# Odd attention: the query norm as scale and bias of the exponential, per partition, instead of spread over the heads' dimensions

## What is computed

```python
def rms_norm(x, g):
    return x * rsqrt(mean(x * x, -1) + EPS) * g

q, k = rms_norm(q, g_q), rms_norm(k, g_k)          # over the 64 dimensions of a head
score = einsum(relu(qi . ki), wi)                  # a small indexer
idx = top_k(score, 256)                            # the keys that a query may see
logits = einsum(q, k[idx]) * 64 ** -0.5            # 8 query heads, 2 key heads
p = softmax(where(sel_ok, logits, NEG))
out = einsum(p, v[idx])
```

## Time and profile before

| | us |
|---|---|
| median of 3 runs | 2625.73 (2623.49 to 2625.83) |
| profiled execution, its own time | 2626.03 |
| its span | 2624.2 |
| PE busy | 2550.2 (97%) |
| DVE busy | 1195.1 (46%) |
| POOL busy | 1087.1 (41%) |
| ACT busy | 598.9 (23%) |

### The profile page before, as it was taken

The page is one execution under the profiler, slowest core; times in us unless marked ns, Lnnn a source line. Parts: engine busy times, 40 slices in busy tenths (PEclk is TensorE's granted clock), DMA queues, the critical chain, the costliest instruction groups (busy, mean ns, idle before and its releaser), DMA issues.

```text
span 2624.2 us, 38744 instructions
## 1 busy us (share of the span) xinstructions
PE 2550.2 (97%) x16483; PEld 2413.7 (92%) x16483; DVE 1195.1 (46%) x1582; ACT 598.9 (23%) x889; POOL 1087.1 (41%) x899
## 2 busy tenths in 40 slices
PE   7999999999999999999989999989999999999998
PEld 7998866999999999999969987669999999999998
DVE  4224389443333323333568876663433343333324
ACT  3200178211001000010248801651200100001000
POOL 5242256344443344443342333953544334443331
PEclk8999999999999999999999998999999999999999
DMA  5111120211111111111040111002111111111101
GB/s 201 49 33 42 46 93 1 83 49 49 40 40 48 48 48 48 42 38 48 21 143 17 49 49 38 18 17 99 49 33 47 48 48 48 46 34 47 48 32 67
DMA packets 93114, 134.13 MB, mean 51 GB/s; under 512 B 13214, under 2 KB 78838, under 8 KB 92503
## 3 DMA queue, kind: packets, MB, share of 16 engines
q1 hardware_dynamic: 90374, 115.40, 13.6%
q10 hardware_dynamic: 2640, 17.31, 1.7%
HBM read 113.16 MB, written 18.73 MB: 50 GB/s over the span
## 4 chain that ended last, share of the span: by engine, by line
PE 88%; ACT 5%; DVE 3%; POOL 1%; issue 1%; DMA 0%; SPq 0%; DVEq 0%; ACTq 0%
PE PS L246 77%; ACT reach L1316 4%; PE PS L962 1%; PE PS L901 1%; PE PS L1267 1%; PE PS L939 1%; PE PS L1296 1%; PE PS L1236 1%; POOL Lb L1612 1%; PE PS L588 1%; DMA xtok<-in_x_prompt 0%; DVE score L1403 0%; PE PS L906 0%; PE PS L1142 0%; DVE h L425 0%
## 5 line engine op out<-in xcount | busy, mean ns | idle before, releaser
L1803 POOL TENSOR_TENSOR w_sp<-stage,ones 128x512 fp32r<-128x512 f32 x372 | 386.3, 1070 | 1368.5 <-PE PS L246 1326.2
L246 PE MATMUL PS<-h,w_sp 128*128 128x352 f32 (+1 forms) x5256 | 873.3, 326 | 18.0 <-DVE h L535 6.6
L246 PEld LDWEIGHTS PS<-h,w_sp 128*128 128x128 f32 (+1 forms) x5256 | 856.4, 190 | 25.1 <-issue 16.6
L246 PE MATMUL PS<-hid,w_sp 128*128 128x352 f32 x4608 | 749.0, 323 | 0.0
L246 PEld LDWEIGHTS PS<-hid,w_sp 128*128 128x128 f32 x4608 | 744.7, 188 | 0.0
L246 PE MATMUL PS<-hz,w_sp 128*128 128x352 f32 x3456 | 567.7, 323 | 0.0
L246 PEld LDWEIGHTS PS<-hz,w_sp 128*128 128x128 f32 x3456 | 558.7, 188 | 0.0
L1807 POOL TENSOR_TENSOR w_sp<-stage,w_sp 128x512 fp32r<-128x512 f32 x372 | 523.0, 1438 | 0.0
L337 DVE TENSOR_TENSOR xT<-PS,xT 128x1056 f32<-128x1056 f32 x248 | 311.5, 1256 | 345.1 <-PE PS L246 345.1
L303 ACT ACTIVATE rbuf<-rbuf 128x1056 f32<-128x1056 f32 x64 | 69.7, 1089 | 1234.2 <-DVE rbuf L327 1234.2
L327 DVE SCALAR_TENSOR_TENSOR rbuf<-PS,rstd 128x1056 f32<-128x1056 f32 x64 | 80.5, 1257 | 505.4 <-PE PS L246 505.3
(11 more groups left out here) (271 smaller groups left out, 1581.7 us busy)
## 6 DMA issues: line engine op xcount, KB each, us to landing
stage<-in_w_ffn SPq DMA_DIRECT2D x64, 1024.0 KB, 5.1
stage<-in_w_in_even SPq DMA_DIRECT2D x10, 1024.0 KB, 5.0
stage<-in_w_in_odd SPq DMA_DIRECT2D x9, 1024.0 KB, 5.1
x_spill<-xT ACTq DMA_DIRECT2D x2, 4224.0 KB, 12.1
xT<-x_spill ACTq DMA_DIRECT2D x2, 4224.0 KB, 12.5
xtok<-in_x_prompt SPq DMA_DIRECT2D x8, 512.0 KB, 8.7
stage<-in_w_out_even SPq DMA_DIRECT2D x4, 1024.0 KB, 8.8
stage<-in_w_out_odd SPq DMA_DIRECT2D x4, 1024.0 KB, 4.8
```

The lines of the kernel that those rows point to most:

```text
L246: mm = pe.matmul(out[0:m, c, :], lhs, rhs(k, b)[:, c * CH:(c + 1) * CH], start=(i == 0 and n == 0), stop=(i == nk - 1 and n == 2))
L1803: pool.tensor_tensor(w_sp[:, s, 0, q:q + 512], stage[:, s, q:q + 512], ones[:, 0:1].to_broadcast([P, 512]), ALU.mult).then_inc(w_hi_done, 1)
```

## The change

The query's tiles are no longer normed. ACT evacuates them with the query's gain as scale, and squares them straight from PSUM. The root is no longer spread over the dimensions of the query's heads (the keys' spread stays). Instead, PE turns the roots (`r_o`, ahead of the reciprocal) with nine small products, so that each query has its heads' roots on its own partition; DVE takes their reciprocals into the table `rT`. In the attention the exponential gets `rT` as its scale, and its bias is minus the maximum times `rT`, which a new product on DVE makes for both heads of a pair (semaphore `c_bias`). The minimum of negated logits becomes a maximum.

```diff
         def pe_odd_spread(pe):
-            for t in range(5):
-                j = J_OR + t
-                pe.wait_ge(set_free[j % 2], j // 2)
-                for c in range(NCH):
-                    mm = pe.matmul(psz(j)[:, c, :], spread5[:, t, :], r_o[:, c * CH:(c + 1) * CH], start=True, stop=True)
-                mm.then_inc(job_done, 1)
+            pe.wait_ge(set_free[J_OR % 2], J_OR // 2)
+            for c in range(NCH):
+                mm = pe.matmul(psz(J_OR)[:, c, :], spread5[:, :], r_o[:, c * CH:(c + 1) * CH], start=True, stop=True)
+            mm.then_inc(job_done, 1)
+
+        def pe_head_turns(pe):
+
+            evacuated(pe, J_OS)
+            each = ident[:, :].rearrange("p (t r) -> p t r", t=4)[:, :, 0:2]
+            for i in range(NTT):
+                c0, m = tok(i)
+                mm = pe.matmul(PS[0:m, 6, 8 * i:8 * i + 8].rearrange("p (t e) -> p t e", t=4), r_o[:, c0:c0 + m], each,
+                               start=True, stop=True)
+            mm.then_inc(r_tp, 1)
...
-            gemm_in_unit(pe, U_OIN + 7, J_OIN + 11)
+            pe.wait_ge(w_split, U_OIN + 8)
+            gemm_tile(pe, J_OIN + 11, (U_OIN + 7) % 2, KT, 0, 256, P, hh)
+            gemm_tile(pe, J_OIN + 12, (U_OIN + 7) % 2, KT, P, 256, P, hh, between=lambda: pe_head_turns(pe), at_k=1)
...
-                if t != 5:
-                    j = OJ[t]
-                    act.wait_ge(job_done, j + 1)
+                j = OJ[t]
+                act.wait_ge(job_done, j + 1)
+                if t < 5:
+                    act.activation(tri3(Z[:, O_SQ[t], :]), psz(j), ACT.Square).then_inc(zsq, 1)
+                if t < 4:
+                    act.activation(tri3(Z[:, OT[t], :]), psz(j), ACT.Copy, scale=gv[:, G_QC:G_QC + 1]).then_inc(set_free[j % 2], 1)
+                elif t != 5:
                     act.activation(tri3(Z[:, OT[t], :]), psz(j), ACT.Copy).then_inc(set_free[j % 2], 1)
-                if t < 5:
-                    evacuated(act, OJ[t])
-                    act.activation(Z[:, O_SQ[t], :], Z[:, OQ + t, :], ACT.Square).then_inc(zsq, 1)
...
+            act.wait_ge(r_td, 2)
             for it in range(NPAIR + 2):
...
+                    act.wait_ge(c_b, it + 1)
                     for e in range(2):
                         t = 2 * it + e
-                        x = Lb[0:m, t % 6, 0:n]
-                        act.wait_ge(c_m, t + 1)
-                        act.activation(x, x, ACT.Exp, scale=-1.0, bias=st[0:m, 0, t:t + 1],
+                        x, hd = Lb[0:m, t % 6, 0:n], 8 * b + t % 8
+                        act.activation(x, x, ACT.Exp, scale=rT[0:m, hd:hd + 1], bias=st[0:m, 3, t:t + 1],
                                        accum_out=st[0:m, 1, t:t + 1]).then_inc(c_e, 1)
...
+            dve.wait_ge(r_tp, 1)
             dve.reciprocal(r_o, r_o).then_inc(zr, 1)
-            ch.link(dve.memset(spread5[:, :, :], 0.0))
-            for t in range(4):
-                r = slice(32 * t, 32 * t + 32)
-                ch.mark(dve.tensor_copy(spread5[r, t, :], spread[r, :]))
-            ch.sync()
+            ch.link(dve.memset(spread5[:, :], 0.0))
...
-            dve_scale(dve, OQ, G_QC, J_OR, 4)
-            dve_scale(dve, OK, G_KC, J_OR + 4, 1)
+            dve_scale(dve, OK, G_KC, J_OR, 1)
+            dve.wait_ge(r_tp, 1)
+            for m, a, b in ((P, 0, 64), (TS, 64, 72)):
+                dve.reciprocal(rT[0:m, a:b], PS[0:m, 6, a:b]).then_inc(r_td, 1)
...
-                        dve.tensor_tensor_reduce(Lb[0:m, t % 6, 0:n], banks(2 * e, n, m), mask, -HD ** -0.5, 3e38,
-                                                 ALU.add, ALU.min, st[0:m, 0, t:t + 1]).then_inc(c_m, 1)
+                        dve.tensor_tensor_reduce(Lb[0:m, t % 6, 0:n], banks(2 * e, n, m), mask, HD ** -0.5, -3e38,
+                                                 ALU.add, ALU.max, st[0:m, 0, t:t + 1]).then_inc(c_m, 1)
+                    dve.wait_ge(c_m, 2 * it + 2)
+                    hd = 8 * b + 2 * (it % 4)
+                    dve.scalar_tensor_tensor(st[0:m, 3, 2 * it:2 * it + 2], st[0:m, 0, 2 * it:2 * it + 2], -1.0,
+                                             rT[0:m, hd:hd + 2], ALU.mult, ALU.mult).then_inc(c_b, 1)
```

More of the change, by code:

```diff
@@ L67 @@
 J_OR = J_OIN + 15
-J_OOUT = J_OIN + 24
+J_OOUT = J_OIN + 20
 J_F1 = J_OOUT + 8
@@ L120, in build_encoder @@
         crow = at("crow", o_f + 2560, [36, 2, P])
+        rT = at("rT", o_f + 1024, [P, 8 * NTT])
         G_MIX, G_FFN, G_QA, G_KA, G_VB, G_QC, G_KC, G_CW = 0, 16, 32, 33, 34, 38, 39, 40
@@ L1070, in build_encoder @@
         sel_done = sem("sel_done")
-        spread5 = zslot("spread5", 9, [P, 5, P])
+        spread5 = zslot("spread5", 9, [P, P])
         O_SQ = [17, 18, 19, 20, 9]
         r_o = Z[:, 10, :]
+        r_tp, r_td, c_b = sem("r_turned"), sem("r_tables"), sem("c_bias")
         OT = [0, 1, 2, 3, 4, 5, 13, 14, 15, 16, 17, 18, 19, 20, 9, 10, 11, 12]
-        OJ = [J_OIN + j for j in (0, 1, 2, 3, 4, 5, 6, 7, 8, 9, 11, 12, 13, 14, 20, 21, 22, 23)]
+        OJ = [J_OIN + j for j in (0, 1, 2, 3, 4, 5, 6, 7, 8, 9, 11, 12, 13, 14, 16, 17, 18, 19)]
         cand_set, act_count = sem("cand_set"), sem("act_count")
@@ L1188, in pe_odd @@
             pe_odd_sums(pe)
-            gemm_in_unit(pe, U_OIN + 7, J_OIN + 11)
+            pe.wait_ge(w_split, U_OIN + 8)
+            gemm_tile(pe, J_OIN + 11, (U_OIN + 7) % 2, KT, 0, 256, P, hh)
+            gemm_tile(pe, J_OIN + 12, (U_OIN + 7) % 2, KT, P, 256, P, hh, between=lambda: pe_head_turns(pe), at_k=1)
             gemm_in_unit(pe, U_OIN + 8, J_OIN + 13)
             pe_odd_spread(pe)
-            gemm_in_unit(pe, U_OIN + 9, J_OIN + 20)
-            gemm_in_unit(pe, U_OIN + 10, J_OIN + 22)
+            gemm_in_unit(pe, U_OIN + 9, J_OIN + 16)
+            gemm_in_unit(pe, U_OIN + 10, J_OIN + 18)
             evacuated(pe, J_OOUT - 1)
@@ L1486, in dve_odd @@
             evacuated(dve, J_OS)
+            dve.wait_ge(r_tp, 1)
             dve.reciprocal(r_o, r_o).then_inc(zr, 1)
-            ch.link(dve.memset(spread5[:, :, :], 0.0))
-            for t in range(4):
-                r = slice(32 * t, 32 * t + 32)
-                ch.mark(dve.tensor_copy(spread5[r, t, :], spread[r, :]))
-            ch.sync()
+            ch.link(dve.memset(spread5[:, :], 0.0))
             for rows, half, x in ((4, 1, 1.0), (3, 1, 0.0), (3, 0, 1.0)):
-                ch.link(dve.memset(spread5[0:rows, 4, 64 * half:64 * half + 64], x))
-            dve.memset(spread5[0:2, 4, 0:64], 0.0).then_inc(sp4, 1)
+                ch.link(dve.memset(spread5[0:rows, 64 * half:64 * half + 64], x))
+            dve.memset(spread5[0:2, 0:64], 0.0).then_inc(sp4, 1)
             out(OJ[11], Z[:, OT[11], :], s_r2)
@@ L1541, in dve_odd @@
             dve.memset(cinp[:, :, 0:2], 0.0).then_inc(cv_done, 1)
+            dve.wait_ge(r_td, 2)
             ch.link(dve.memset(m01[:, :, :], 0.0))
@@ L1647, in sp_odd @@
             sp_.wait_ge(sel_done, 1)
-            evacuated(sp_, J_OR + 4)
+            evacuated(sp_, J_OR)
             sp_.dma_start(kS[64:128, :], Z[0:64, OK, :]).then_inc(ks_in, 16)
@@ L1785, in last_job @@
                     n = u - U_OIN
-                    return J_OI + 2 * n + (1 if n in (0, 7, 8) else 6 if n > 8 else 0)
+                    return J_OI + 2 * n + (1 if n in (0, 7, 8) else 2 if n > 8 else 0)
                 u0, j0 = (U_F0, J_F0) if u < U_OIN else (U_F1, J_F1)
```

## The result

The changed kernel takes 2647.8 us (median of 5 runs, 2640.4 to 2653.9) where the one before takes 2625.7: 1.0082 times as long, 95% interval 1.0068 to 1.0096. I had forecast 2626.7, with a range from 2621.0 to 2632.5: wrong, on the slower side.

The account below looks back on a forecast made before the run. PE was taken to bound the kernel (88% of the chain of waits), with ACT beside it in the search. Terms -7.1 + 1.7 - 0.6 + 5.8 + 1.2 = +1.0 gave 2626.7 us by the median, range 2621 to 2632.5.

Parts of the forecast that it names:

- The projection: Odd layer's input projection: four spreads gone, head turns added, squares from PSUM; -7.1 + 1.7 - 0.6 us.
- the spreads: Projection, PE: products spreading roots over the heads' dimensions; four of five go at 1.78 us each, -7.1 us.
- the head turns: Projection, PE: nine new products of 8 columns inside a gemm tile, 18 records at 0.09, +1.7 us.
- squares and copies: Search beside the projection, ACT: squares straight from PSUM save time, scaled copies cost some; -0.6 us, bounds 0 and -1.
- The product's price: Attention, DVE: new 128 x 2 product of maximum and root, priced by the same-shape reciprocal at 0.17 us.
- my upper end of the loop: Attention: bound of +8 us on the longer loop, if wide pairs lose 0.1 or 0.2 each.
- the ring: Attention: 36 pairs of heads going round scores, mask and maximum, exponential, reciprocal, scaling, turns and values.
- the hidden loop: Attention rival: POOL or PE sets the pace, so DVE's added wait falls into idle time; 2621 us, chance 0.18.
- The loop: Attention: maximum, product, exponential, reciprocal, next maximum; 3.4 us instead of 2.82 at pair 13, +5.8 us over pairs 8 to 23.
- The clock: Attention rival: longer loop idles PE, so its clock falls again between pairs 8 and 23; +9 in all, 2635 us, chance 0.10.
- The price of 8 us for half rate: Attention, PE: 17 us of a second low-clock stretch at half rate lose 8 us of work.
- The start: Attention's first exponential: table load stands behind the wait for the product, 1.8 us late; +1.2 us taken, bounds 0 and 1.8.

Follow-up runs that it names:

- e3: Kernel before, plus one product of two 128 x 2 SBUF tensors on DVE per pair that nobody waits for: 2635.2 us, ratio 1.0040.
- e1: Changed kernel with each pair's product made by two one-column instructions, the root as a scalar per partition instead of a second tensor: 2634.9 us, ratio 1.0039.
- e6: Changed kernel with its two-tensor product, but POOL's convolution operations in the attention shrunk to one column (output left out): 2635.2 us, ratio 1.0037.
- e5: e1 plus two spare 128 x 128 products on PE behind the values of each of the pairs 8 to 20: 2631.1 us, ratio 1.0024.
- e4: Changed kernel's projection with the attention of the kernel before; the query stays without its norm: 2621.1 us, ratio 0.9983.
- e10: e1 plus one spare one-column exponential on ACT ahead of the attention's pairs, so the table loads beside the first scores: 2635.3 us, ratio 1.0040.
- e2: Changed kernel without the product: exponential's bias is a column of zeros, and exponentials wait for both maxima of the pair: 2628.1 us, ratio 1.0007.
- e7: Changed kernel without maximum and product: DVE multiplies scores by the root while adding the mask; each exponential waits for its own head: 2617.4 us, ratio 0.9976.
- e9: Changed kernel with a one-column product per head directly behind its maximum, root as scalar per partition; exponentials wait for their own: 2623.9 us, ratio 0.9994.
- e11: e9 with each head's product made from two tensors in SBUF instead of one tensor and a scalar per partition: 2649.4 us, ratio 1.0092.

## Why the prediction was wrong

**The projection** was right: -7.1 for the spreads (8.76 - 1.67), 2.0 for the head turns (I said 1.7), -0.6 for squares and copies (from the first gemm tile to the last copy of the search it is 127.88 before and 127.28 after). That is -5.7, where I had -6.0. The -7.0 between the two traces holds more than the change: in the 47 us behind the search PE was granted 0.97 before, and 1.00 after, which is some 1.4 us of its time. The windows before and after:

```profile
1513.00:1560.00 47.00, 47.00 (x286) 47.00 (x285) 36.57 (x70) 0.32 (x1) 11.54 (x8) 0.97 0.14 45
```

```profile
1510.00:1557.00 47.00, 47.00 (x298) 46.96 (x297) 34.95 (x64) 0.00 (x0) 11.54 (x8) 1.00 0.14 45
```

The projection of before, run again in e3, has 1.00 there and takes 236.8 us, not 238.1; the changed one has a stretch at the low clock there in e1 and takes 232.7, not 231.1. Like with like the gain is 5.4 to 5.6 us.

**The product's price** is the step that failed. I wrote that it "is priced by the reciprocal of the same shape, 0.17". The reciprocal reads one tensor in SBUF, the product reads two, and that decides beside a busy POOL. What this cost was 13 us by e1 (which has one instruction more a pair), 17 by e6 (which relieves POOL), and I had no bound for it: my upper end of the loop, +8, held no such case. The trace of before had rows that warn of it. Selections of the mask are products of two tensors in SBUF as well (lines 1508 and 1509): on DVE first those of a block of 768 keys, then those of the sample's 544,

```profile
1574.30 1.02 DVE L1508 SCALAR_TENSOR_TENSOR Z<-Z,bs__66 128x768 f32<-128x768 f32 x1
1575.35 0.96 DVE L1509 SCALAR_TENSOR_TENSOR score<-Z 128x768 f32<-128x768 f32 x1
...
1598.26 1.64 DVE L1508 SCALAR_TENSOR_TENSOR Z<-Z,bs__66 32x544 f32<-32x544 f32 x1
1599.93 1.70 DVE L1509 SCALAR_TENSOR_TENSOR score<-Z 32x544 f32<-32x544 f32 x1
```

and POOL beside them:

```profile
1592.84 4.24 POOL L1803 TENSOR_TENSOR w_sp<-stage,ones 128x512 fp32r<-128x512 f32 x4 [23.14 <-PE PS L246]
1597.04 6.99 POOL L1807 TENSOR_TENSOR w_sp<-stage,w_sp 128x512 fp32r<-128x512 f32 x4
```

POOL is idle beside the first two and splits weights from 1592.84 to 1604.03, beside the last two. The narrower ones take 1.7 times as long; they end 0.6 us behind the ends of two of POOL's operations (1599.32 and 1601.05), about the time that 544 columns need. For the ring I had noted POOL as "busy without a break in the pairs 9 to 20", and took it for an argument for the hidden loop. It is what holds the products. The Trainium skill says it, page "SBUF — State Buffer", section "Who interferes with whom": an instruction of VectorE with two SBUF inputs contends with a GpSimd instruction that reads SBUF, and the one that comes second waits until the first has ended. The traces here agree (ends 0.01 and 0.02 us apart in the two cases shown), and show more: in both cases the product lost to POOL's next operation as well. I had weighed two other rules of the Trainium skill and not this one, which spoke against the change.

**The loop** was right, in kind and in size. Where its product isn't held, pair 13 of the changed kernel takes 3.41 us from maximum to maximum, and I had 3.4:

```profile
1650.96 0.69 DVE L1575 CUSTOM_DVE_ANT_0 Lb<-PS,score 128x512 f32<-128x512 f32 x1
...
1652.31 0.17 DVE L1579 SCALAR_TENSOR_TENSOR st<-st,rT 128x2 f32<-128x2 f32 x1
...
1654.25 0.17 DVE L1565 RECIPROCAL st<-st 128x2 f32<-128x2 f32 x1 [1.31 <-ACT Lb L1370]
1654.37 0.69 DVE L1575 CUSTOM_DVE_ANT_0 Lb<-PS,score 128x512 f32<-128x512 f32 x1
```

In e6, which holds none, pairs that the low clock leaves alone take 2.97 us at 384 columns, 3.40 at 512, 3.49 at 544 and 3.88 at 640. Four of each are 55.0 us, where I had 54.4 for pairs 8 to 24: +6.4 instead of +5.8. So the mean width could stand for all. From pair 24 on e6 takes 53.8, as before: nothing, as I said. e1 and e5 take 0.16 more a pair (3.57 at pair 13) for their second instruction, 2.6 of the 57.7 that e5 needs from 8 to 24.

**The clock** was a rival with 0.10, and came true on top of the loop; the sign that I had named for it, a granted clock under 1.00 behind 1645, is there. My argument against it, that the clock had stayed at 1.00 with 3.98 of 5 us busy in the last pairs and that the loop leaves PE 90%, did not carry: in e1 it fell behind windows with 3.93 and 4.08, 80% of the ten us. It needs no long loop either: in e3 the spare products are enough. The price of 8 us for half rate was too high: some 3.6.

**The start** was +1.2 in my sum. For the pairs 0 to 8 the changed kernel has +3.0, but e4, with the attention of before, already has +1.9: it is granted 0.50 there for some 20 us (about 1616 to 1636), where before it was 17. The changed kernel has the same 20 us, and 1.1 more than e4. So the start itself was about right, and not much of it is the table load (0.5 by e10). Why the first stretch at the low clock is longer stays open: e2 and e7, with the same projection, have 17 us.

Together: -5.7 in the projection, +1.1 at the start and +6.4 in the loop make +1.8, where I had +1.0. What I did not have is 13 to 17 for the products that POOL holds, some 3.6 for the second stretch at the low clock and 1.9 that goes with the longer first one. That is +20 to +24, and +22.1 was measured. The parts come from differences between single traces and overlap somewhat (a held product also leaves PE idle), so the sum is a check of size and no more.

## What to carry to other kernels

Before a small instruction is put into a ring, look at where its operands lie and which engine is busy beside it; price it by a row with the same operands, not the same shape. A scalar per partition in place of a second tensor took 13 us (e1) and 25 us (e9 against e11) out of this kernel. This is shown for products of one column only. In the trace of before, an operation with one tensor and scalars per partition (line 1506) takes 0.61 us for 768 columns beside an idle POOL, and over twice that for 544 beside its weight splits:

```profile
1571.86 0.61 DVE L1506 TENSOR_SCALAR Z<-score,bs__66 128x768 f32<-128x768 f32 x1
...
1594.85 1.33 DVE L1506 TENSOR_SCALAR Z<-score,bs__66 32x544 f32<-32x544 f32 x1
```

If an engine's result is waited for by a pair, see whether the first of the two can go on alone: e9 has as many instructions as e1 and is 11 us faster.

## What the runs showed of the hardware

A product of 128 x 2 on DVE with both tensors in SBUF takes 0.15 to 2.5 us in the same kernel, 2.9 in e3, depending on what POOL runs beside it. It can lose to the operation that POOL runs and to the next one too: the one at 1666.40 did, while the one at 1662.91, which began 0.10 us before POOL's scaling ended, took 0.15.

The same product with one tensor and a scalar per partition is never held: 0.19 to 0.22 us for all 72 in e1, and 0.20 to 0.22 in e9, where most begin while an operation of POOL runs.

PE's busy time in 5 us did not tell by itself whether the granted clock would fall. In the changed kernel it stayed at 1.00 from 1710 to 1715 us with 2.94 of 5 us busy, and fell behind 1665 to 1670 with 2.67; in e1 it fell behind 3.93 and 4.08.
